# A final norm made inside the last expert pass, and a first weight split taken ahead of a square

## The reference, cut to what matters

```python
h = x
hn = rmsnorm(h, norm_mix_g)
proj = hn @ w_in                      # 1024 x 1024 by 1024 x 2568
mix = concatenate([s5_mixer(...), mlstm_mixer(...)])
h = h + mix @ w_out
h = h + moe_ffn(rmsnorm(h, norm_ffn_g), w_router, ..., w_up, b_up, w_down, b_down)
return rmsnorm(h, norm_final_g)

def rmsnorm(x, g):
    return x * rsqrt(mean(x * x, axis=-1) + 1e-5) * g

# an expert, for the rows xb that chose it
h = xb @ w_up[e] + b_up[e]
g = minimum(h[:, :F], 7.0); lin = clip(h[:, F:], -7.0, 7.0)
y = (g * sigmoid(1.702 * g) * (lin + 1.0)) @ w_down[e] + b_down[e]
```

## Time and profile before

| what | value |
|---|---|
| time, median of 3 runs | 2331.73 us (2330.88 to 2335.7) |
| time of the profiled execution | 2334.58 us |
| its span | 2332.8 us |
| PE busy | 2165.6 us (93%) |
| DVE busy | 1628.8 us (70%) |
| ACT busy | 1214.0 us (52%) |
| POOL busy | 558.7 us (24%) |
| mean granted TensorE clock | 0.961 of full |

### The profile page before, as it was taken

One profiled execution on the slowest core, in us unless ns is written; L12 is line 12 of the kernel. 1 busy time (PEld: TensorE's weight loads), 2 busy tenths in 40 slices (PEclk: granted clock), 3 DMA queues, 4 the chain that ended last, 5 costly groups with the idle time before them and its releaser, 6 DMA issues. The chain is left out here.

```text
span 2332.8 us, 32427 instructions
## 1 busy us (share of the span) xinstructions
PE 2165.6 (93%) x10466; PEld 1800.8 (77%) x10467; DVE 1628.8 (70%) x1862; ACT 1214.0 (52%) x1241; POOL 558.7 (24%) x539
## 2 busy tenths in 40 slices
PE   6999876889589999999999999999999999999993
PEld 5787876668378888888888888888888888888872
DVE  4688756646775665768678785778875787686774
ACT  4422233233164554657467574766755576565653
POOL 1001221102520111305125131522511252121401
PEclk9999967999589999999999999999999999999997
DMA  6123261541395676869779886988996798687974
GB/s 177 55 82 140 79 126 45 171 167 55 132 380 206 229 233 197 292 233 358 264 269 371 306 287 216 316 305 280 365 318 197 251 367 311 227 278 263 314 233 179
DMA packets 285812, 540.81 MB, mean 232 GB/s; under 512 B 37154, under 2 KB 53586, under 8 KB 284658
## 3 DMA queue, kind: packets, MB, share of 16 engines
q1 hardware_dynamic: 260306, 490.51, 59.9%
q0 software_dynamic: 25440, 49.47, 8.2%
HBM read 513.06 MB, written 64.57 MB: 248 GB/s over the span
## 5 line engine op out<-in xcount | busy, mean ns | idle before, releaser
L2402 DVE TENSOR_TENSOR ex_w_lo<-ex_raw,ex_w_hi 128x2048 fp32r<-128x2048 f32 x408 | 926.7, 2289 | 373.2 <-ACT ex_w_hi L2295 306.5
L2295 ACT CAST ex_w_hi<-ex_raw 128x2048 fp32r<-128x2048 f32 x371 | 706.7, 1911 | 278.8 <-PE ex_ps_g L2611 99.8
L2206 POOL TENSOR_TENSOR ex_passed<-ex_ident 128x1 f32<-128x1 f32 x136 | 134.0, 985 | 1183.6 <-ACT ex_y L2338 1152.6
L2610 PE MATMUL ex_ps_g<-ex_w_hi,ex_x_hi 128*128 128x512 f32 x784 | 307.4, 392 | 8.4 <-issue 6.5
L2610 PE MATMUL ex_ps_l<-ex_w_hi,ex_x_hi 128*128 128x512 f32 x784 | 308.8, 394 | 1.2 <-DVE ex_w_lo L2402 1.2
L2611 PE MATMUL ex_ps_g<-ex_w_lo,ex_x_hi 128*128 128x512 f32 x784 | 305.5, 390 | 0.0
L2611 PE MATMUL ex_ps_l<-ex_w_lo,ex_x_hi 128*128 128x512 f32 x784 | 305.3, 389 | 0.0
L2610 PE MATMUL ex_ps_y<-ex_w_hi,ex_h_hi 128*128 128x512 f32 x544 | 217.1, 399 | 0.6
L2614 PE MATMUL ex_ps_g<-ex_w_hi,ex_x_lo 128*128 128x512 f32 x544 | 212.3, 390 | 0.0
L2614 PE MATMUL ex_ps_l<-ex_w_hi,ex_x_lo 128*128 128x512 f32 x544 | 212.0, 390 | 0.0
L2611 PE MATMUL ex_ps_y<-ex_w_lo,ex_h_hi 128*128 128x512 f32 x544 | 211.9, 390 | 0.0
(11 more groups left out here) (464 smaller groups left out, 3746.9 us busy)
## 6 DMA issues: line engine op xcount, KB each, us to landing
ex_raw<-in_w_up_dram SPq DMA_DIRECT2D x272, 1024.0 KB, 8.7
ex_raw<-in_w_down_dram SPq DMA_DIRECT2D x136, 1024.0 KB, 8.1
st_tab<-tabs SPq DMA_DIRECT2D x8, 1408.0 KB, 7.3
pr_raw<-in_w_in_dram SPq DMA_DIRECT2D x10, 1024.0 KB, 5.4
tabs<-pr_x POOLq DMA_DIRECT2D x32, 256.0 KB, 2.3
por_raw<-in_w_out_dram SPq DMA_DIRECT2D x16, 256.0 KB, 4.7
t<-mix_sig_o SPq DMA_DIRECT2D x8, 512.0 KB, 2.6
fi_h<-h SPq DMA_DIRECT2D x8, 512.0 KB, 7.6
```

Of the source, the lines that this page charges most:

```text
L2206: pool.tensor_tensor(passed[:, :], ident[:, 0:1], ident[:, 0:1], ALU.add).then_inc(passed_done, 1)
L2295: nc.scalar.copy(w_hi[:, j % SPLIT, :, :], raw[:, j % RAW, :, :]).then_inc(hi_done, 1)
L2402: v.tensor_tensor(w_lo[:, j % SPLIT, :, :], raw[:, j % RAW, :, :], w_hi[:, j % SPLIT, :, :].bitcast(F32), ALU.subtract).then_inc(lo_done, 1)
L2610: pe.matmul(to[:, :], hi_in[:, b, kk, :], w_hi[:, s, k, :], start=first, stop=False)
```

## The change

In `project`, the square, mean and norm of tile 2 are placed behind the first weight's cast on ACT and behind its subtraction on DVE.

`finish` is gone. Its work is done in `experts`, during the last pass:

- SP, after its last weight load, loads the gain (into `bias_rows`, whose rows are no longer needed), waits until the y of the pass before has landed in `h`, and loads tiles 0 to 3 of `h`; when chunk 7 of the last pass is split, tiles 4 to 7 follow (the later ones into raw buffers 0 and 1). Then it stores each tile when it is scaled.
- ACT squares tiles 0 and 1 at j = 6, 2 and 3 at j = 7, 4 to 7 at j = 8, each time behind the work that it had there.
- POOL gathers the last pass's own rows of `h` into `x_rows`, makes the powers of tiles 0 to 3 and 4 to 7, two instructions for four tiles each, issues the last accumulating scatter into `h` as before, makes the power of the rows, issues the second scatter, and when all tile stores have landed writes the finished rows over them by an indirect DMA (plain, no accumulation), for whose landing it waits.
- DVE scales tiles 0 to 4 in place, waits for y, adds y to the gathered rows, scales tiles 5 to 7, and scales the rows.

All eight tiles are normed with `h` as it was ahead of the last pass's y; the rows to which that y belongs are then normed by themselves and written last. Where there are later passes (`most` > 384), all tiles are loaded, normed and stored again.

```diff
@@ project, ACT
                     if j == 1:
                         hi(0)
-                    if j + 2 < TT:
+                        square(2)
+                    if 1 <= j < TT - 2:
                         square(j + 2)
@@ project, DVE
-                    if j + 1 < TT:
+                    if j + 1 < TT and j != 1:
                         norm(j + 1)
...
                     if j == 1:
                         lo(0)
-                    if j + 2 < TT:
+                        mean(2)
+                        norm(2)
+                    if 1 <= j < TT - 2:
                         mean(j + 2)
@@ experts, SP
+                def norm_all_but_last(n):
+                    sp.wait_ge(bias_set, 2)
+                    sp.dma_start(final_gain, ...).then_inc(final_gain_in, 16)
+                    for b in range(PAIR):
+                        sp.wait_ge(y_free[b], n * 16 + 16)
+                    for j in range(TT):
+                        if j == 4:
+                            sp.wait_ge(lo_done, n * CHUNKS + (LOW + RAW_USED))
+                        final_load(j)
+                    for j in range(TT):
+                        final_store(j, 0)
+                    sp.wait_ge(stored, 16 * TT)
@@ experts, POOL
+                def power(part, done):
+                    pool.wait_ge(squared, done)
+                    pool.tensor_scalar(mean[:, part], mean[:, part], RMS_EPS, None, ALU.add).then_inc(eps_added, 1)
+                    pool.wait_ge(eps_added, 1 + done // 4)
+                    pool.tensor_tensor(rstd[:, part], mean[:, part], neg_half[:, :], ALU.pow).then_inc(rstd_set, 1)
+                def last_pass(n, at, turn, blocks):
...
+                    pass_on(turn + 1)
+                    for b in range(blocks):
+                        pool.indirect_dma_start(out=x_rows[:, b, :], in_=h3_dram, ...).then_inc(back_in[b], 16)
+                    power(slice(0, 4), 4)
+                    power(slice(4, 8), 8)
+                    pool.wait_ge(y_a_read, n + 2)
+                    pool.wait_ge(y_b_read, n + 2)
+                    carry_on(1)
+                    for j in range(TT):
+                        pool.wait_ge(final_in[j], 16)
+                    for b in range(blocks):
+                        pool.wait_ge(back_in[b], 16)
+                    add_rows(0, blocks)
+                    pool.wait_ge(row_squared, blocks)
+                    pool.tensor_scalar(row_mean[:, 0:blocks], ...).then_inc(row_eps_added, 1)
+                    pool.wait_ge(row_eps_added, 1)
+                    pool.tensor_tensor(row_rstd[:, 0:blocks], ..., ALU.pow).then_inc(row_rstd_set, 1)
+                    add_rows(1, blocks)
+                    pool.wait_ge(row_done, blocks)
+                    pool.wait_ge(stored, 16 * TT)
+                    for b in range(blocks):
+                        pool.indirect_dma_start(out=out_rows, in_=x_rows[:, b, :], ...).then_inc(rows_out, 16)
+                    pool.wait_ge(rows_out, 16 * blocks)
@@ experts, ACT, in item
+                        if kind is LAST and j in (6, 7, 8):
+                            for t in range(4 if j == 8 else 2):
+                                square(2 * j - 12 + t, 0)
+                    if kind is LAST:
+                        for b in range(blocks):
+                            square_row(b)
@@ experts, DVE, at the end of item when kind is LAST
+                def norm_all_but_last(n, blocks):
+                    v.wait_ge(final_gain_in, 16)
+                    for j in range(5):
+                        scale(j, 0)
+                    v.wait_ge(y_a_read, n + 2)
+                    v.wait_ge(y_b_read, n + 2)
+                    for b in range(blocks):
+                        v.wait_ge(back_in[b], 16)
+                        v.tensor_tensor(x_rows[:, b, :], x_rows[:, b, :], y[:, b, :], ALU.add).then_inc(row_added, 1)
+                    for j in range(5, TT):
+                        scale(j, 0)
+                    v.wait_ge(row_rstd_set, 1)
+                    for b in range(blocks):
+                        v.scalar_tensor_tensor(x_rows[:, b, :], x_rows[:, b, :], row_rstd[:, b:b + 1], final_gain,
+                                               ALU.mult, ALU.mult).then_inc(row_done, 1)
@@ hybrid_block
-        experts(nc, p, t, h3, keep)
-        finish(nc, p, h3, out)
+        experts(nc, p, t, h3, keep, out)
```

More of the change, by code:

```diff
@@ L1999, in _, with experts @@
                     add_bias(j)
-def experts(nc, p, t_dram, h3_dram, keep):
+def experts(nc, p, t_dram, h3_dram, keep, out):
     with ExitStack() as ctx:
@@ L2150, in last_passes, with more_items @@
                 body(n + (plan & 1), e, 1, plan, LAST)
-        def more_items(eng, body):
+        def more_items(eng, body, end=None):
             most = eng.value_load(keep["most"][0:1, 0:1], min_val=0, max_val=T)
@@ L2164, in more_items @@
                             body(n + 1, e, w, 1)
+                if end is not None:
+                    end()
         with nc.Block() as block:
@@ L2188, in later @@
                         load(n, e, j)
-                more_items(sp, later)
+                more_items(sp, later, norm_again)
             @block.gpsimd
@@ L2196, in _ @@
                 pool.memset(ident[:, :], 0.0).then_inc(ident_set, 1)
+                pool.memset(neg_half[:, :], -0.5).then_inc(eps_added, 1)
                 pool.wait_ge(ident_set, 1)
@@ L2274, in later, with norm_again @@
                             pool.wait_ge(y_free[b], n * 16 + 32)
-                more_items(pool, later)
+                def norm_again():
+                    carry_on(2)
+                    pool.wait_ge(carried, 2)
+                    pool.sem_inc(all_added, 1)
+                    power(slice(0, 4), TT + 4)
+                    power(slice(4, 8), TT + 8)
+                more_items(pool, later, norm_again)
                 plan = pool.value_load(keep["plan"][0:1, E - 1:E], min_val=1, max_val=8 * 2 * E + 7)
@@ L2393, in later, with norm_again @@
                     item(n, ALONE, blocks)
-                more_items(act, later)
+                def norm_again():
+                    for j in range(TT):
+                        square(j, 1)
+                more_items(act, later, norm_again)
             @block.vector
@@ L2528, in later, with norm_again @@
                     item(n, ALONE, blocks, e, None)
-                more_items(v, later)
+                def norm_again():
+                    for j in range(TT):
+                        scale(j, 1)
+                more_items(v, later, norm_again)
             @block.tensor
```

176 lines of the change are left out of this document (107 added, 69 removed).

## The result

| | before | after |
|---|---|---|
| median of 5 runs of each, same chip (us) | 2332.03 (2330.88 to 2335.70) | 2320.72 (2317.58 to 2322.48) |
| profiled execution (us) | 2334.58 | 2321.82 |
| its span | 2332.8 | 2320.1 |
| mean granted TensorE clock | 0.961 | 0.965 |

The ratio of the changed kernel's time to that of the one before is 0.9948, with a 95% interval of 0.9934 to 0.9963: by the medians the change makes the kernel 11.3 us faster. Forecast were 16.8, so about two thirds of it came. The median is 0.2 us above the upper end of the range; the ratio times the 2331.73 that the forecast started from is 2319.6, inside it. The profiled spans differ by 12.7 us. What follows finds the missing 4 us.

The account below looks back on a forecast made before the run. It took the bare final norm as the bound, 37.0 us after the last y with TensorE idle, and TensorE's wait at the start. Start 3.2 plus tail 13.6 made 16.8 off 2331.73: 2314.9 us, range 2310 to 2320.5.

Parts of the forecast that it names:

- Start, 3.2 less: In project: with tile 2's work behind the first weight, the first matmul begins at 18.8 for 22.02, 3.2 us less.
- start gives little: Rival, chance 0.10: at the start a landing (weight 1, tile 4) becomes the bound, shift 0 to 1 us; about 2317.5.
- Loads and squares: Last pass: tile loads after SP's last weight, squares on ACT; cost 1.1 us on the last y, tile 0 0.5 early.
- wrong if a square waits for a load: Sign for the last pass: no DMA wait on ACT before the eight squares, else the prediction is wrong.
- Other edits cost nothing: Remaining edits, such as finish's memset and barriers falling away, larger buffers and an untaken norm_again, were to add no time.
- the slower rival: Rival, chance 0.02: longer program fetched worse at each of 31 expert loop turns; at 0.8 us each, 2339.7.
- Second power: Last pass, tiles 4 to 7: POOL's add and power come after DVE's scales end at 2295.9 and take 0.8 us.
- Last store: Tail: the last tile store lands 4.3 us after the scales end at 2303.1, so at 2307.4.
- Rows' write: Tail: POOL's indirect write, issued from 2307.8, lands in 5.0 us, at 2312.8; 4.0 and 5.6 kept for the range.
- Way out: After the write's landing: POOL's register loads 1.9, DRAIN 3.74, closing barriers 0.75 us; end at 2319.2.
- DRAIN might count from the landing: Way out: if DRAIN's time runs from the landing, the register loads hide in it and 1.9 us comes back.
- the dear end: Rival, chance 0.20: tile 0 lands 2 to 3 us late, write 5.6 or more, rows' power 2 late; 2318.4.

Follow-up runs that it names:

- e1: The kernel before with the edit of the start in project alone, finish kept; median 2329.88 us for 2332.59, ratio 0.9988.
- e8: The changed kernel with the last pass's two-block version placed behind the one-block version that runs; 2325.45 us beside 2337.76 of before, ratio 0.9951.
- e10: The changed kernel with SP awaiting the rows' write, empty add early, two-block version behind one-block, final gain loaded behind tile 3; 2323.38 us, ratio 0.9924.
- e6: The changed kernel with the empty add into h issued early and the add of the last y into h left out; 2325.25 us, ratio 0.9944.
- e3: The changed kernel with SP in place of POOL waiting for the rows' write to land; median 2318.36 us, ratio 0.9940.

## Why the prediction was right or wrong

By the profiled execution 12.7 us came where 16.8 were forecast. Point by point:

- **Start, 3.2 less: right.** 3.3 at the first matmul, 3.1 still at 276 us in the profiled execution. The rival "start gives little" has happened too, in four of eleven profiles, by the clock and not by the landing that it names; the median of e1 gives the half alone 2.8.
- **Loads and squares: right in size, in part by luck.** The squares cost 1.0 for 1.1. But tile 0 was not there 0.5 us ahead of ACT: it came at 2280.28, 0.25 late, where 2281.7 less the 2.2 of shift was forecast, so that "wrong if a square waits for a load" is met. Without that wait the loss would have been some 0.75, below the 1.1, and 0.6 of it was the entry's already. The mechanism (the hidden rows' cast behind four squares) is the one of the text, and "if it is late, every step above is late with it" is what e8 and e10 show.
- **Entry: missing.** "Other edits cost nothing" doesn't count the longer code, and the slower rival looked for a fetch stall at the 31 turns of the expert loop. Its count of instruction transfers, 35 in all, is that of one queue; the page has a second (q14, 31 packets). The stall, whatever is waited for in it, sits at one place outside the loop, the jump into the last pass over a version that has become longer: 3.5 us of ACT, 1.6 of TensorE.
- **Second power: right in kind.** Its add was ready only during the fourth scale, was held by that scale, and the power came after it; DVE idle 1.25 for 0.8, made up by the scales that repeat every 1.20.
- **Last store, "lands 4.3 later": wrong, 6.4.** 4.3 was taken from finish, where no add ran beside the store. The text itself has the accumulate begin at 2297.3 and calls it "hidden too". It was hidden as work of POOL, but it shared the DMA engines with the last store: without it, 4.4 (e6). 2.1 of the miss.
- **Rows' write, 5.0: 1.4 too much.** It landed in 3.6, below the lower bound of 4.0. The estimate by the Trainium skill, "DMA: Bandwidth & Descriptors" ("Anatomy of one DMA — SWDGE (gpsimd) path"), was 3.2, nearer to the 3.6 than the 5.0 that was taken; in all eleven profiles the write lands in 3.3 to 3.9. This error hid part of the others.
- **Way out, 1.9 + 3.74 + 0.75: 2.3 too little.** From the write's landing to DRAIN 3.8 passed and not 1.9, of which 1.45 are one gap between two register operations; DRAIN 3.91; closing 1.0. That DRAIN might count from the landing is refuted by e3.

The tail's terms in sum: -0.3 for the scales, +2.1 for the store, +0.4 for the way to the write's issue, -1.4 for the write, +2.3 for the way out: 3.1, with which 22.3 becomes 25.4. Add 1.6 on entry, take off 0.2 for start and squares and 0.5 by which the stages between ran ahead: 4.0 of the 4.1 by which the span missed 2316.0. Of the rivals the dear end is the nearest by its time and by one of its reasons (transfers that share the engines), though it looked for them at tile 0 and at the write.

The range holds the time with some luck. The terms that it names lead from 2314.9 down to 2311.2 (write 1.0, DRAIN 1.9, start 0.8) and up to 2319.2 (write 0.6, ACT 2.0, start 1.7), not to 2310 and 2320.5. Both 2319.6, by the ratio, and 2320.7, the median, lie above 2319.2, and they would lie higher had the write not been 1.4 us cheaper than forecast.

## What to carry to other kernels

Put a wait for a landing on the engine that has nothing to do behind it: the same wait moved from POOL to SP took 3.6 us off, since POOL's register loads and a fixed DRAIN of 3.9 stood in line behind it. A transfer hidden from its engine is not hidden from the stores that it flies beside: cost it on the DMA engines as well. When an edit makes a block of code longer, look at the engines' first instruction behind the jump over it. If it stands behind idle time put down to "issue", moving the block that isn't carried out is worth a trial; read the rest of the trace then too, since here the move took 1.5 us off the entry, and with it the last store landed in 6.8 to 7.6 us instead of 6.4 to 6.5.

## What was not expected of the hardware

- DRAIN on POOL's queue after software DMAs had a fixed length from where it begins: 3.907 us in ten of the eleven profiles that end the new way, whether it began 3.8 us behind the write's landing or during its flight; 3.826 in e6, with one transfer less.
- A gap of 1.3 to 1.7 us among POOL's register operations ahead of DRAIN in all eleven of these profiles, with an 8 KB instruction transfer that starts in it or up to 0.3 us ahead of it. The kernel before has such a transfer too, at 2298.54, but POOL waits there for a scatter's landing until 2302.55, so that a gap would be hidden.
- TensorE's granted clock after the same 2.17 us of waiting fell to 1.2 GHz in some executions (0.54 over two us in e1) and stayed at 2.4 GHz (1.00) in others of the same code.
- The accumulating software DMA took 57.7% of the engines' time for 35 packets where 37 packets of a plain store took 42.2%.
- The kernel before needs 2332.0, 2332.6, 2337.8 and 2340.8 us in the four sets of runs, on at least three chips, and the ratio holds all the same.
